# First RMSNorm of a decoder layer: x laid out by channel on the host, sums of squares and spread factors as TensorE products in place of transposes

## What is computed

```python
def rmsnorm(x, w):
    xf = x.astype(jnp.float32)
    y = xf * lax.rsqrt(jnp.mean(xf * xf, axis=-1, keepdims=True) + EPS)
    return (y * w.astype(jnp.float32)).astype(x.dtype)
...
z = rmsnorm(x, norm1_w) @ w_in
hq, hf, hi, hg, dq, dk, dv, ga, gb = split_cols(z)
```

## Time and profile before

| | |
|---|---|
| three runs, us | 1719.77, 1724.35, 1724.97; median 1724.35 |
| the profiled execution, us | 1728.1 |
| its span in the profile, us | 1726.3 |
| TensorE busy | 1547.2 us, 90% |
| VectorE busy | 707.1 us, 41% |
| ScalarE busy | 461.9 us, 27% |
| GpSimd busy | 235.8 us, 14% |
| mean granted TensorE clock | 0.941 of full |

### The profile page before, as it was taken

One profiled execution on the slowest core, in us unless ns is written; L12 is line 12 of the kernel. 1 busy time (PEld: TensorE's weight loads), 2 busy tenths in 40 slices (PEclk: granted clock), 3 DMA queues, 4 the chain that ended last, 5 costly groups with the idle time before them and its releaser, 6 DMA issues. The chain is left out here.

```text
span 1726.3 us, 22053 instructions
## 1 busy us (share of the span) xinstructions
PE 1547.2 (90%) x7497; PEld 1056.2 (61%) x7498; DVE 707.1 (41%) x1465; ACT 461.9 (27%) x1040; POOL 235.8 (14%) x417
## 2 busy tenths in 40 slices
PE   5999999986899898989789999999799929999996
PEld 3566565665465565655568888888678724444442
DVE  4368886886244453444432222233332241222121
ACT  2233343332233343334332222122232200111110
POOL 1000111011222222222100000000000001122221
PEclk8999999987799998989889999999999959999998
DMA  7001200000402001000055667233343392987973
GB/s 243 26 0 59 78 1 26 1 27 1 143 1 63 1 30 35 1 27 1 27 168 183 199 198 251 80 110 110 132 118 110 110 316 76 336 240 227 302 206 49
DMA packets 119369, 186.03 MB, mean 108 GB/s; under 512 B 9507, under 2 KB 82262, under 8 KB 117222
## 3 DMA queue, kind: packets, MB, share of 16 engines
q1 hardware_dynamic: 107750, 134.41, 24.4%
q0 software_dynamic: 11520, 50.34, 10.0%
HBM read 154.38 MB, written 30.34 MB: 107 GB/s over the span
## 5 line engine op out<-in xcount | busy, mean ns | idle before, releaser
L972 PE MATMUL psum<-attention_part,kept 128*128 128x384 f32 (+1 forms) x576 | 205.6, 513 | 0.7 <-DVE attention_part L1205 0.7
L2166 PE MATMUL psum<-moe_part,kept 128*128 x384 | 172.3, 602 | 6.4 <-issue 4.9
L972 PEld LDWEIGHTS psum<-attention_part,kept 128*128 128x128 f32 (+1 forms) x576 | 110.2, 196 | 78.7 <-issue 20.9
L1438 PE MATMUL psum<-split 128*128 128x368 f32 x384 | 140.6, 366 | 2.5 <-DVE split L1584 2.5
L498 PE MATMUL psum<-kept,recurrence_part 128*128 128x368 f32 x384 | 124.7, 480 | 10.0 <-PEq L236 5.0
L1427 PE MATMUL psum<-kept,sample_part 128*128 128x368 f32 x384 | 131.8, 487 | 1.3 <-PEq L873 1.3
L1440 PE MATMUL psum<-split 128*128 128x368 f32 x384 | 127.3, 332 | 0.0
L2166 PEld LDWEIGHTS psum<-moe_part,kept 128*128 128x128 f32 x384 | 72.3, 193 | 89.6 <-issue 89.6
L1439 PE MATMUL psum<-split 128*128 128x368 f32 x384 | 127.0, 331 | 0.0
L503 PE MATMUL psum<-recurrence_part,kept 128*128 128x512 f32 (+1 forms) x288 | 125.9, 593 | 0.0
L1593 DVE TENSOR_TENSOR merge_part<-merge_part,psum 128x368 f32<-128x368 f32 x48 | 25.8, 538 | 220.2 <-ACT merge_part L1527 220.2
(11 more groups left out here) (312 smaller groups left out, 2527.3 us busy)
## 6 DMA issues: line engine op xcount, KB each, us to landing
sample_part<-merge_gates POOLq DMA_DIRECT2D x16, 1024.0 KB
merge_part<-cache_kT SPq DMA_DIRECT2D x64, 256.0 KB, 3.4
merge_part<-cache_v SPq DMA_DIRECT2D x64, 256.0 KB, 3.1
moe_part<-w_gate SPq DMA_DIRECT2D x16, 1024.0 KB, 6.2
moe_part<-w_up SPq DMA_DIRECT2D x16, 1024.0 KB, 12.6
moe_part<-w_down SPq DMA_DIRECT2D x16, 1024.0 KB, 14.0
recurrence_part<-w_in SPq DMA_DIRECT2D x8, 1024.0 KB, 9.2
sample_part<-merge_out POOLq DMA_DIRECT2D x16, 512.0 KB, 6.4
```

The lines of the kernel that those rows point to most:

```text
L972: mm = pe.matmul(bank_of(("z", h, i))[:ROWS[i], 0:384], K["xT"][:, k, cols(i)], Wb[h % 2][:, k, :], start=(k == 0), stop=(k == KC - 1))
L1438: pe.matmul(bank_of(u, 2 * j + 1), wh[w % 2][:, k, ch], xh[b][:, k, :], start=(k == 0), stop=False)
L2166: mm = pe.matmul(psum[:, 2 + par, :], XT[par][:, k, :], K["GU"][:, bass.ds(KC * b + k, 1), :], start=(k == 0), stop=(k == KC - 1))
```

## The change

The host hands over x a second time, as `xT`: channels on the partitions, tile by tile, each tile contiguous within a partition; and the vectors as one array `vectors` of 128 x 19. So x arrives in the layout that `K["xT"]` has, and no transpose is left in the phase. What was a sum along a row is now a sum over partitions and chunks, which TensorE makes: ScalarE squares the tile elementwise into `sq` (L275), and eight products with the squares as stationary operand and one column of ones as moving operand add up in PSUM to a column with one sum for each token (L378). VectorE makes mean + EPS out of it (L301), GpSimd raises it to -0.5 (L294). Since tokens lie along the free axis, the factor must stand in every partition: VectorE multiplies the identity by the column (`diag`, L308), and TensorE multiplies an all-ones matrix by that diagonal matrix (L369), which leaves the 128 factors in each partition of PSUM. The channel weights are multiplied in apart from that: by GpSimd for even tiles (L291), by VectorE for odd ones (L312). At last VectorE multiplies the tile in place by the spread factors (L321).

All nine tiles have buffers of their own, so their loads wait for nothing. Block 0 of the recurrence weights is issued right behind them, ahead of the small constants, block 1 behind the constants. Line numbers of the changed kernel are those of the order listings below.

```diff
@@ -236,13 +236,14 @@
+        vec_in, const_in, setup = sem("vec_in"), sem("const_in"), sem("setup")
+        x_in = [sem(f"x_in{i}") for i in range(NT)]
+        squared, summed, mean_done, rstd_done, spread, rstd_wide, weighted = (sem(n) for n in (
+            "squared", "summed", "mean_done", "rstd_done", "spread", "rstd_wide", "weighted"))
+        scaled = sem("scaled")
+        lb_max, lb_exp, lam_dot, lam_exp = sem("lb_max"), sem("lb_exp"), sem("lam_dot"), sem("lam_exp")
+        xin, sq = [sb(KC, P) for _ in range(NT)], [sb(KC, P) for _ in range(2)]
+        mean, rstd, power, ones, diag = sb(NT), sb(NT), sb(NT), sb(P), sb(2, P)
...
@@ -250,40 +251,28 @@
 
         @block.sync
         def _(sp):
-            sp.dma_start(K["ident"], A["ident"]).then_inc(const_in, 16)
-            for r0, n, src in ((0, 8, A["norm1_w"].rearrange("a (r c) -> (a r) c", c=P)),
-                               (8, 8, A["hg_lb_logits"].rearrange("a (r c) -> (a r) c", c=P)),
-                               (16, 1, A["hg_onorm_w"]), (17, 1, A["da_onorm_w"])):
-                sp.dma_start(rows[r0:r0 + n, :], src).then_inc(rows_in, 16)
-            for m in range(2):
-                sp.dma_start(rows[18:19, 64 * m:64 * m + 64], A["q_norm_w"]).then_inc(rows_in, 16)
+            sp.dma_start(vec, A["vectors"]).then_inc(vec_in, 16)
+            sp.dma_start(K["ident"], A["ident"]).then_inc(vec_in, 16)
             for i in range(NT):
-                if i >= 3:
-                    sp.wait_ge(xn_done, i - 2)
-                if i == 0:
-                    sp.dma_start(xin[0:META, 0, :], A["meta_tokens"]).then_inc(x_in[0], 16)
-                    sp.dma_start(xin[META:FIRST, 0, :], A["x_sample"].rearrange("a b d -> (a b) d")).then_inc(x_in[0], 16)
-                else:
-                    sp.dma_start(xin[:, i % 3, :], A["x_prompt"][0, P * (i - 1):P * i, :]).then_inc(x_in[i % 3], 16)
+                sp.dma_start(xin[i].rearrange("p a b -> p (a b)")[:, 0:KC * ROWS[i]], A["xT"][:, KC * COL[i]:KC * (COL[i] + ROWS[i])]).then_inc(x_in[i], 16)
+            load_recurrence_block(sp, A, K, 0)
             sp.dma_start(lp.rearrange("p a b -> p (a b)"), A["da_lambda"].rearrange("a b c -> a (b c)").to_broadcast([P, 256])).then_inc(const_in, 16)
             sp.dma_start(K["knorm"], A["k_norm_w"].to_broadcast([P, 64])).then_inc(const_in, 16)
             sp.dma_start(K["combine"], A["combine"]).then_inc(const_in, 16)
             sp.dma_start(K["table"][0:1, :], A["page_table"].rearrange("a b -> (a b)").unsqueeze(0)).then_inc(const_in, 16)
-            load_recurrence_block(sp, A, K, 0)
             load_recurrence_block(sp, A, K, 1)
-            sp.wait_ge(const_in, 80)
+            sp.wait_ge(const_in, 64)
+
+        def x_of(i):
+            return xin[i].rearrange("p a b -> p (a b)")[:, 0:KC * ROWS[i]].rearrange("p (a b) -> p a b", b=ROWS[i])
 
         @block.scalar
         def _(act):
             for i in range(NT):
-                x_ready(act, i)
-                if i:
-                    act.drain()
-                act.activation(junk[:ROWS[i], :], xin[:ROWS[i], i % 3, :], ACT.Square,
-                               accum_out=ssq[:ROWS[i], i:i + 1]).then_inc(ssq_done, 1)
+                act.wait_ge(x_in[i], 16)
+                if i >= 2:
+                    act.wait_ge(summed, i - 1)
+                act.activation(sq[i % 2][:, :, :ROWS[i]], x_of(i), ACT.Square).then_inc(squared, 1)
...
         @block.gpsimd
         def _(pool):
+            pool.memset(ones, 1.0).then_inc(setup, 1)
             pool.memset(power, -0.5).then_inc(setup, 1)
             pool.memset(K["half"], -0.5).then_inc(setup, 1)
-            pool.wait_ge(setup, 2)
+            pool.wait_ge(setup, 3)
+            pool.wait_ge(vec_in, 32)
             for i in range(NT):
+                if i % 2 == 0:
+                    pool.wait_ge(x_in[i], 16)
+                    pool.tensor_tensor(K["xT"][:, :, cols(i)], x_of(i), vec[:, 0:KC].unsqueeze(2).to_broadcast([P, KC, ROWS[i]]), ALU.mult).then_inc(weighted, 1)
                 r = ROWS[i]
-                pool.wait_ge(ssq_done, i + 1)
-                pool.tensor_scalar(mean[:r, i:i + 1], ssq[:r, i:i + 1], 1.0 / D, EPS, ALU.mult, ALU.add)
-                pool.drain()
+                pool.wait_ge(mean_done, i + 1)
                 pool.tensor_tensor(rstd[:r, i:i + 1], mean[:r, i:i + 1], power[:r, i:i + 1], ALU.pow).then_inc(rstd_done, 1)
 
         @block.vector
         def _(dve):
-            def evacuate(i):
+            def average(i):
                 r = ROWS[i]
-                dve.wait_ge(turned, i + 1)
-                dve.tensor_tensor(K["xT"][:, :, cols(i)], psum[:, 2 * (i % 2):2 * (i % 2) + 2, :].rearrange("p a (b c) -> p (a b) c", c=P)[:, :, :r],
-                                  vec[:, 0:8].unsqueeze(2).to_broadcast([P, KC, r]), ALU.mult).then_inc(evacuated, 1)
-
-            for i in range(NT):
+                dve.wait_ge(summed, i + 1)
+                dve.tensor_scalar(mean[:r, i:i + 1], psum[:r, i % 4, 0:1], 1.0 / D, EPS, ALU.mult, ALU.add).then_inc(mean_done, 1)
+
+            def place(i):
                 r = ROWS[i]
-                x_ready(dve, i)
                 dve.wait_ge(rstd_done, i + 1)
                 if i >= 2:
-                    dve.wait_ge(turned, i - 1)
-                dve.tensor_scalar(xn[:r, i % 2, :], xin[:r, i % 3, :], rstd[:r, i:i + 1], None, ALU.mult).then_inc(xn_done, 1)
-                if i == 0:
-                    dve.wait_ge(vec_turned, 1)
-                    dve.tensor_copy(vec, psum[:, 4, 0:19])
+                    dve.wait_ge(rstd_wide, i - 1)
+                dve.tensor_scalar(diag[:r, i % 2, :r], K["ident"][:r, :r], rstd[:r, i:i + 1], None, ALU.mult).then_inc(spread, 1)
+
+            def weigh(i):
+                dve.wait_ge(x_in[i], 16)
+                dve.tensor_tensor(K["xT"][:, :, cols(i)], x_of(i), vec[:, 0:KC].unsqueeze(2).to_broadcast([P, KC, ROWS[i]]), ALU.mult)
+
+            def scale(i):
+                dve.wait_ge(rstd_wide, i + 1)
+                if i % 2:
                     dve.drain()
                 else:
-                    evacuate(i - 1)
-            evacuate(NT - 1)
+                    dve.wait_ge(weighted, i // 2 + 1)
+                x = K["xT"][:, :, cols(i)]
+                dve.tensor_tensor(x, x, psum[:, 4 + i % 4, 0:ROWS[i]].unsqueeze(1).to_broadcast([P, KC, ROWS[i]]), ALU.mult).then_inc(scaled, 1)
+
+            dve.wait_ge(vec_in, 32)
+            for i in range(NT + 2):
+                if i < NT and i % 2:
+                    weigh(i)
+                if i < NT:
+                    average(i)
+                if 1 <= i <= NT:
+                    place(i - 1)
+                if i >= 2:
+                    scale(i - 2)
 
...
@@ -354,18 +361,26 @@
 
         @block.tensor
         def _(pe):
-            pe.wait_ge(const_in, 16)
-            pe.wait_ge(rows_in, 96)
-            pe.transpose(psum[:, 4, 0:19], rows[0:19, :], K["ident"][0:19, 0:19]).then_inc(vec_turned, 1)
+            def spread_out(i):
+                r = ROWS[i]
+                pe.wait_ge(spread, i + 1)
+                if i >= 4:
+                    pe.wait_ge(scaled, i - 3)
+                pe.matmul(psum[:, 4 + i % 4, 0:r], ones[:r, :], diag[:r, i % 2, :r], start=True, stop=True).then_inc(rstd_wide, 1)
+
+            pe.wait_ge(setup, 1)
             for i in range(NT):
                 r = ROWS[i]
-                pe.wait_ge(xn_done, i + 1)
+                pe.wait_ge(squared, i + 1)
+                if i >= 4:
+                    pe.wait_ge(mean_done, i - 3)
+                for k in range(KC):
+                    mm = pe.matmul(psum[:r, i % 4, 0:1], sq[i % 2][:, k, :r], ones[:, 0:1], start=(k == 0), stop=(k == KC - 1))
+                mm.then_inc(summed, 1)
                 if i >= 2:
-                    pe.wait_ge(evacuated, i - 1)
-                for k in range(KC):
-                    mm = pe.transpose(psum[:, 2 * (i % 2) + k // 4, P * (k % 4):P * (k % 4) + r],
-                                      xn[:r, i % 2, P * k:P * k + P], K["ident"][:r, :r])
-                mm.then_inc(turned, 1)
+                    spread_out(i - 2)
+            for i in (NT - 2, NT - 1):
+                spread_out(i)
...
@@ -2289,6 +2304,12 @@
+    x = np.concatenate([arrays["meta_tokens"], arrays["x_sample"].reshape(NSAMP, D), arrays["x_prompt"][0]])
+    parts = [x[cols(i)].reshape(ROWS[i], KC, P).transpose(2, 1, 0).reshape(P, KC * ROWS[i]) for i in range(NT)]
+    arrays["xT"] = np.concatenate(parts, axis=1)
+    rows = [arrays.pop("norm1_w").reshape(KC, P), arrays.pop("hg_lb_logits").reshape(2 * HEADS, P), arrays.pop("hg_onorm_w"),
+            arrays.pop("da_onorm_w"), np.tile(arrays.pop("q_norm_w"), (1, 2))]
+    arrays["vectors"] = np.concatenate(rows).T.copy()
     arrays.update(constants())
```

(18 more changed lines are left out.)

## The result

The changed kernel takes 1733.49 us (median of 5 runs, 1730.06 to 1735.69) where the kernel before takes 1724.35 on the same chip: ratio 1.0061, 95% interval 1.0040 to 1.0081, so 9.1 us slower by the medians (the interval is 7 to 14 us). The forecast of 1725.3 and its range up to 1729.5 missed it. The profiled execution took 1735.5 us, its span is 1733.8. One execution of the kernel before (2660 us) and the profiled one of e12 (3067 us) ran far slower from end to end than all others; the ratios leave them out.

What follows compares the result with a forecast made beforehand. TensorE was taken to bound the kernel behind the barrier, the VectorE-GpSimd round the first phase. Phase end +0.9 us: span 1726.3 + 0.9 = 1727.2, plus 1.8 is 1729.0, less 3.8 gives median 1725.3 us; range 1719.5 to 1729.5.

Steps and rivals of the forecast that it cites:

- TensorE's sums: First phase: eight one-column products sum a tile's squares, 0.95 us at 2.4 GHz and 1.83 at 1.2; 1.83 was taken.
- the round of VectorE and GpSimd: First phase: weighing, placing, scaling and power in turn set the pace, 5.24 us for two tiles, 5.5 at 1.2 GHz.
- The low clock: TensorE in the first phase: the new stream is thinner than the earlier one, so 1.2 GHz was taken for the sums.
- The third rival: First phase: load and product do not overlap, TensorE becomes the bound, 4.0 us a tile, end 44.5, kernel 1737; 5%.
- The exclusion of VectorE and GpSimd: First phase: VectorE steps with two SBUF inputs or tensor_scalar from SBUF exclude GpSimd steps; a PSUM input is free.
- The start: First phase: GpSimd weighs tile 0 from 8.36, the second weighing starts at 10.9, the last at 26.2.
- the 6.9 that stood beside it: GpSimd's start in the first phase if its first call to fresh code costs 5.95 us; end then 31.8.
- the lower bound of 5.1: Earliest start of GpSimd's first weighing, when the first tile of x has loaded; end then 31.6.
- Loads and constants: First phase: x tiles at about 5.1 and 6.5, others at most 2.1 us apart; weight loads and constants stay hidden.
- the rival of a late start at 10.4: First phase: GpSimd's first weighing comes late; at 10.4 the end is 34.1, kernel 1726.6; 15%, a third beyond 0.3%.
- The sum: Whole kernel: phase end 32.8 against 31.88, +0.9 us; 1729.0 against the profiled 1728.1, 1725.3 as a median.
- a us at the barrier is a us of the kernel: Premise: TensorE is the limit behind the first phase's barrier, so a later opening reaches the kernel's end in full.

Runs made afterwards that it cites:

- e12: The changed kernel with 128 columns of ones in float32 sums, constants moved to mid-phase and 23 idle float32 products before the barrier; 1722.5 us (before 1722.9).
- e2: The changed kernel with each of the eight sum products writing its own PSUM column and VectorE adding them; 1733.8 us (before 1724.4), ratio 1.0061.
- e4: The changed kernel with all nine weighings on VectorE and none on GpSimd; 1733.6 us (before 1724.4), ratio 1.0068.
- e1: The changed kernel with the sums' products reading 128 columns of ones instead of one, still float32; 1721.7 us (before 1724.4), ratio 0.9993.
- e3: The changed kernel with squares and a pair of columns of ones written as float32r; 1723.3 us (before 1724.4), ratio 0.9998.
- e5: The changed kernel with squares and ones in float32r and 128 columns of ones; 1726.5 us (before 1724.6), ratio 1.0013.
- e9: The kernel before with ten idle VectorE multiplications behind the last L309, so the barrier opens later; 1734.8 us (before 1722.9), ratio 1.0072.
- e7: The changed kernel with float32r sums of 128 columns, no weighing (scale fused into eight VectorE steps) and constants moved to mid-phase; 1727.5 us (before 1724.6).
- e11: The kernel before with 18 idle float32 products of 128 columns behind its last transposes; 1723.3 us (before 1722.9), ratio 1.0012.
- e10: e7 plus 23 idle float32 products of 128 columns between the last sums and the barrier; 1716.8 us (before 1722.9), ratio 0.9962.
- e8: e7 plus 40 idle float32r products of 128 columns between the last spreads and the barrier; 1727.1 us (before 1724.6), ratio 1.0018.

## Why the prediction was wrong

*TensorE's sums: the step that failed.* The prediction read the earlier trace rows as 18 products, 0.23 each, and took eight products for 8 x 0.23 = 1.83. Those 18 records are nine products of two records each (L1902 makes 2 x 9 products, and the earlier trace rows counts 36 records), and eight float32 products are sixteen records: 16 x 0.213 = 3.41 (e2, e4 and after alike). The earlier trace rows was misread in the same way: a tile's sum at the high clock is 1.95 (e1), not 0.95. With 1.83 TensorE lay under the round of VectorE and GpSimd, with 3.41 it sets the pace. e3 shows the pair by taking one of the two away, and nothing else: 1.85 for x8. The low clock, the other factor, was forecast rightly, but by luck, from a wrong picture: the stream was to be thinner than the one of the earlier trace rows, and it was dense, TensorE being busy without a gap from 6 to 38 us, and stayed at 1.2 GHz nevertheless.

*The third rival* had the size: 3.4 for the sums, 4.0 a tile, end at 44.5, kernel 1737, against 3.41, 3.84, 42.7 and 1733.5. It had the mechanism wrong (loads and products that do not overlap, where they do: 333 ns of load and 346 of product every 213), and 5% of the chance. That its 0.42 for a product is nearly two records of 0.213 is chance: 0.42 was the length of a single record. Its evidence against, the 0.23 spacing, was the misread row.

*The exclusion of VectorE and GpSimd* was right and did not matter: it is seen in e1, e3 and e5 (L308 held to 1.08 beside L291), where TensorE is out of the way. The round was put at 5.24 and is 4.9: GpSimd begins its weighing while VectorE still scales from PSUM, so VectorE is held for 0.8 of the 1.9 us, and its own steps fill the rest. In the changed kernel TensorE's 3.84 covers it (e4). By the Trainium skill (SBUF — State Buffer, SBUF: two separate sides) the port pair is an exclusive lock; the trace agrees, with L321 at its usual 1.22 beside L291 and L308 at 1.08 for 0.27.

*The start.* The first weighing was taken at 8.36 and began at 5.34, released by the load of x and ahead of the 6.9 that stood beside it; the lower bound of 5.1 was the right end. The first power was 1.49 long for 0.55, beside VectorE's L312, and ended 0.45 after it. Nothing was won by it, since the sums decide.

*Loads and constants*: right. ScalarE had the first tile at 5.19 (5.1 forecast) and waited 0.5 us for the second, at 6.44 (6.5 forecast); no engine waited for a later one, L513 was released by the barrier, and L351, which needs the constants, did not wait. Two slips of the working changed nothing: 512 KB at 220 GB/s are 2.4 us, not 2.1, and the rival of a late start at 10.4 was counted from 32.0 and not from the forecast's 32.8.

*The sum.* Late barrier 11.1 us for 0.9. That a us at the barrier is a us of the kernel held to within 2 us (e9, with some 4 us of scatter). With 3.41 for the sums and 0.43 for the spread TensorE sets the pace at 3.84, the last L321 ends at 42.7, 10.8 us later than L309 did, and the prediction's own sum gives 1735.

## What to carry to other kernels

What an edit at the start wins or loses can be given back far behind it (3.7 us at one store in e7), so look for the same instruction in both traces before a gain or a loss is put down to the place of the edit.

## What the runs showed of the hardware

- Records 0.213 apart did not all do the same to the clock. It rose in e1 (float32, 128 columns) at 10.3 us, and behind idle float32 products of 128 columns in e11 (begun at 31.0, risen at 35.3) and in e10 (24.6 and 25.9, there right behind float32r sums). It did not rise in 32 us of float32 sums with one column (after, e2, e4), nor with float32r sums of 2 or 128 columns (e3, e5 to e8); all of these have the two records of a float32 spread of 128 columns among those of each tile.
- The clock stayed high over the barrier where TensorE's gap was 1.4 us (e10) and 0.8 us (e11). No run shows a steadily busy TensorE at the high clock go into a gap of 5 us: before and e9 had lost it at 28.3 and 25.9 us, ahead of their gaps of 5.0 and 18.4, after never had it, and e1, with only three spreads in its last 4.2 us, lost it at 30.8, with the last of them. These four then had 3.1 to 5.0 us of the low clock in the recurrence.
- At 1.2 GHz a record with a full load comes every 0.213 us with 1, 2 or 128 columns (after, e3, e1), at 2.4 GHz every 0.11 with 64 or 128 (e1).
- A 64 KB store with a 16 KB packet of instructions starting about 1 us behind its issue landed at 3.1 to 3.4 us in place of 1.6 (five of 52 stores), and in e7 this cost 3.7 us, by a load that waited and a clock that fell.
